# A two-block transformer kernel: mLSTM scores and FoX denominators on the whole matmul array, and new written-out orders for two stages

## The reference, cut to what matters

```python
def _mixer(h, lb, w_in, b_in, a_q_g, a_k_g, b_conv_w, out_g, w_out):
    z = h @ w_in + b_in
    ...
    oa = _fox_attention(qa, ka, _heads(a_v, A_HEADS), ca)            # 8 heads of 64
    qk = jax.nn.silu(_causal_dwconv(b_qk, b_conv_w))
    ob = _mlstm_chunkwise(...)                                       # 4 heads of 64
    oc = _hgrn2_chunkwise(jax.nn.silu(_heads(c_q, C_HEADS)), logf, _heads(c_i, C_HEADS))  # 4 heads of 64
    ya = _rms(_merge(oa), g_a.reshape(A_HEADS, HEAD_DIM)).reshape(bsz, t, A_DIM)
    ...
    return jnp.concatenate([ya, yb, yc], axis=-1).astype(h.dtype) @ w_out
```

```python
        z = jnp.einsum("bhqd,bhkd->bhqk", qb, kb) * scale
        log_1m = jnp.where(valid, jax.nn.log_sigmoid(-z), 0.0)
        log_a = jax.nn.log_sigmoid(z) + lax.cumsum(log_1m, axis=3, reverse=True) - log_1m
        a = jnp.where(valid, jnp.exp(log_a), 0.0)
        outs.append(jnp.einsum("bhqk,bhkd->bhqd", a.astype(v.dtype), v[:, :, :kend]))
```

## Time and profile before

| what | value |
|---|---|
| median of 3 runs | 1684.35 us (1683.88 to 1684.54) |
| profiled execution | 1683.83 us |
| its span on the core | 1682.1 us |
| PE busy | 1669.3 us (99%), 7812 instructions |
| PE weight loads busy | 1328.1 us (79%) |
| DVE busy | 882.9 us (52%) |
| ACT busy | 661.8 us (39%) |
| POOL busy | 136.8 us (8%) |
| chain that ended last | PE 97%, DVE 2%, ACT 1% |

### The profile page before, as it was taken

One profiled execution on the slowest core, in us unless ns is written; L12 is line 12 of the kernel. 1 busy time (PEld: TensorE's weight loads), 2 busy tenths in 40 slices (PEclk: granted clock), 3 DMA queues, 4 the chain that ended last, 5 costly groups with the idle time before them and its releaser, 6 DMA issues.

```text
span 1682.1 us, 19174 instructions
## 1 busy us (share of the span) xinstructions
PE 1669.3 (99%) x7812; PEld 1328.1 (79%) x7812; DVE 882.9 (52%) x1161; ACT 661.8 (39%) x972; POOL 136.8 (8%) x161
## 2 busy tenths in 40 slices
PE   9999999999999999999999999999999999999999
PEld 7878877788888778888888877777666888888887
DVE  5436744555554354444443337766545677777321
ACT  5344333333553243233222334255574544444211
POOL 0000000121210010000000220212100200000000
PEclk9999999999999999999999999999999999999999
DMA  6222232232453123323323322412203232233321
GB/s 261 88 77 87 76 101 76 76 99 90 163 164 124 38 78 98 94 94 101 98 90 102 99 101 88 164 64 65 74 26 125 88 101 96 93 100 99 102 94 57
DMA packets 47463, 164.28 MB, mean 98 GB/s; under 512 B 5056, under 2 KB 5184, under 8 KB 47056
## 3 DMA queue, kind: packets, MB, share of 16 engines
q1 hardware_dynamic: 46192, 158.88, 28.6%
q0 software_dynamic: 896, 3.70, 0.7%
q10 hardware_dynamic: 288, 0.48, 0.1%
HBM read 158.81 MB, written 4.23 MB: 97 GB/s over the span
## 4 chain that ended last, share of the span: by engine, by line
PE 97%; DVE 2%; ACT 1%; issue 0%; DMA 0%; POOL 0%; SPq 0%; DVEq 0%; ACTq 0%; POOLq 0%
PE pst L382 95%; PE pst L547 1%; PE pst L830 1%; DVE XL L1584 0%; DMA X<-xT 0%; DVE qx L1804 0%; DVE WL L1572 0%; POOL acc L2283 0%; ACT WH L951 0%; DVE ML L1580 0%; PE pst L671 0%; ACT Sx L951 0%; DVE X L1789 0%; PE pst L621 0%; ACT XH L951 0%
## 5 line engine op out<-in xcount | busy, mean ns | idle before, releaser
L382 PE MATMUL pst<-XH,WH 128*128 128x512 f32 x1320 | 528.4, 400 | 0.0
L382 PE MATMUL pst<-XH,WL 128*128 128x512 f32 x1320 | 514.6, 390 | 0.0
L382 PE MATMUL pst<-XL,WH 128*128 128x512 f32 x1320 | 514.2, 390 | 0.0
L1572 DVE TENSOR_TENSOR WL<-raw,WH 128x1024 fp32r<-128x1024 f32 x276 | 341.8, 1239 | 312.3 <-ACT WH L951 311.8
L951 ACT ACTIVATE WH<-raw 128x1024 fp32r<-128x1024 f32 (+1 forms) x278 | 291.3, 1049 | 356.8 <-PE pst L382 351.1
L382 PEld LDWEIGHTS pst<-XH,WH 128*128 128x128 f32 x1320 | 247.8, 188 | 66.4 <-issue 16.5
L382 PEld LDWEIGHTS pst<-XH,WL 128*128 128x128 f32 x1320 | 247.7, 188 | 52.5
L382 PEld LDWEIGHTS pst<-XL,WH 128*128 128x128 f32 x1320 | 248.0, 188 | 51.9 <-issue 3.4
L382 PE MATMUL pst<-HH,WH 128*128 128x512 f32 x352 | 136.9, 389 | 0.0
L382 PE MATMUL pst<-HL,WH 128*128 128x512 f32 x352 | 136.9, 389 | 0.0
L382 PE MATMUL pst<-HH,WL 128*128 128x512 f32 x352 | 136.9, 389 | 0.0
(11 more groups left out here) (252 smaller groups left out, 1789.6 us busy)
## 6 DMA issues: line engine op xcount, KB each, us to landing
raw<-wst SPq DMA_DIRECT2D x276, 512.0 KB, 3.6
X<-xT SPq DMA_DIRECT2D x7, 512.0 KB, 7.2
xs<-X SPq DMA_DIRECT2D x1, 2048.0 KB, 9.3
nC<-cd POOLq DMA_DIRECT2D x4, 512.0 KB, 7.9
X<-xs SPq DMA_DIRECT2D x2, 1024.0 KB, 5.6
outT<-X SPq DMA_DIRECT2D x8, 256.0 KB, 4.4
qx<-memT SPq DMA_DIRECT2D x1, 1024.0 KB, 5.0
gt<-cd POOLq DMA_DIRECT2D x1, 1024.0 KB, 6.3
```

The lines of the kernel that those rows point to most:

```text
L382: return nc.tensor.matmul(out, lhs, rhs, start=start, stop=stop)
L1572: vec.tensor_tensor(WL[:, i % NHL, :], raw[:, i % NRAW, :], WH[:, i % NHL, :].bitcast(F32), ALU.subtract).then_inc(wl, 1)
```

## The change

**Scores over the whole array.** A new tile `kz` holds the keys of each mLSTM head on their own 64 partitions and zeros on the other 64. POOL fills it with zeros once, before it sets `bv1`. The key half of `bqk_silu` on ACT becomes two instructions of 64 partitions that write into `kz`. A score matmul takes all 128 partitions of `kz` and `bqk`. Since `bqk` still holds the second head's queries then, the outputs go to a new tile `yb`.

**Denominators over the whole array.** `den` loses one copy. ACT's square writes every denominator 64 times into `Sx[:, s, 1, :]`, 512 columns instead of 8, and waits first until the last values are read. PE adds them with four matmuls of 128 columns by 128 instead of eight of 64.

**Orders.** `mixer_order` is spelled out, and `heads_order` is another string. The needs are the same.

```diff
-        den = sb("den", [P, 2, 2, 8], stack=st)
+        den = sb("den", [P, 2, 8, 1], stack=st)
+        pad_ = sb("pad_", [P, 11], stack=st)
+        kz = sb("kz", [P, 2, 2, T], stack=st)
+        yb = sb("yb", [P, 2, T], stack=st)
...
-        mixer_order = weave(
-            {"main": (0, 1, mixer_steps), "stick00": (-0.0593, 0.481, 20), ...
+        mixer_order = spelled(
+            "macamamc5mc5mca5maca6mamcma7mca4ma6mcma2ma4ma8ma4mc3mca5ma2mcmc3mcma5ma3macmac5mc5mc4mc6mc7mbc2mb10mdmdb4mdb5m...
...
-            "21mgm2gm2g5mgm2gmg3m2gmg2m2g2mgm2g2mgmgmgmgm2g2m2gmg4m...
+            "22mgm4g7m3gm2g3mg3mg2m2g4m5g2mgmgm2gmgm2g4m2gmgmgmgmgmg2mgmh...
...
                 mm(ps[b1][:, :], halves, Sx[:, s, 0, :], True, False)
                 for x, i in enumerate((3, 2, 1, 0)):
-                    for e in range(2):
-                        d = den[:, s, 1, 2 * x + e:2 * x + e + 1].to_broadcast([P, 64])
-                        ins = mm(ps[b1][64 * e:64 * e + 64, i * P:(i + 1) * P], d, ident, False, x == 3)
+                    ins = mm(ps[b1][:, i * P:(i + 1) * P], Sx[:, s, 1, x * P:(x + 1) * P], ident, False, x == 3)
...
-                            mm(ps[6][:, 0:w], bqk[po:po + 64, 2 + pt, j * P:(j + 1) * P], bqk[po:po + 64, pt, j * P:T]).then_inc(l_p, 1)
+                            pe.wait_ge(ones_ok, 1)
+                            mm(ps[6][:, 0:w], kz[:, pt, h % 2, j * P:(j + 1) * P], bqk[:, pt, j * P:T]).then_inc(l_p, 1)
...
-                        run(ACT.Silu, bqk[:, m, :], bqk[:, m, :]).then_inc(bq_a, 1)
+                        if i == 0:
+                            run(ACT.Silu, bqk[:, m, :], bqk[:, m, :]).then_inc(bq_a, 1)
+                        else:
+                            act.wait_ge(ones_ok, 1)
+                            run(ACT.Silu, kz[0:64, half, 0, :], bqk[0:64, m, :])
+                            run(ACT.Silu, kz[64:P, half, 1, :], bqk[64:P, m, :]).then_inc(bq_a, 1)
...
-                run(ACT.Square, den[:, s, 1, :], den[:, s, 0, :], scale=(64 * EPS) ** 0.5).then_inc(n_a[s], 1)
                 act.wait_ge(f_y[s], 4 * pn + 4)
+                d = Sx[:, s, 1, :].rearrange("p (h d) -> p h d", d=64)
+                run(ACT.Square, d, den[:, s, :, :].to_broadcast([P, 8, 64]), scale=(64 * EPS) ** 0.5).then_inc(n_a[s], 1)
                 run(ACT.Square, Sx[:, s, 0, :], ystk[:, s, :]).then_inc(n_a[s], 1)
...
-                    run(ACT.Copy, bqk[po:po + 64, pt, :], ps[7][0:64, :]).then_inc(l_a, 1)
+                    run(ACT.Copy, yb[po:po + 64, pt, :], ps[7][0:64, :]).then_inc(l_a, 1)
...
+            gp.memset(kz[:, :, :, :], 0.0)
             gp.memset(bv1[:, :, :, 64:P], 1.0).then_inc(ones_ok, 1)
```

More of the change, by code:

```diff
@@ L322, in yy_src @@
         def yy_src(m):
-            return aq[:, m, :] if m < 4 else bqk[:, m - 4, :] if m < 6 else cq[:, m - 6, :]
+            return aq[:, m, :] if m < 4 else yb[:, m - 4, :] if m < 6 else cq[:, m - 6, :]
         Z_SLOT = [4, 5, 6, 7, 0, 1, 2, 3]
         mixer_steps = 2 * (8 + 4 * 2 + 4 * 6 + 4 * 2 + 24 + 24)
-        mixer_order = weave(
-            {"main": (0, 1, mixer_steps), "stick00": (-0.0593, 0.481, 20), "stick01": (0.577, 0.996, 20), "stick10": (-0.0412, 0.676, 20), "stick11": (0.65, 1.01, 20)},
-            {("stick01", 0): (("stick00", 20),), ("stick11", 0): (("stick10", 20),)})
+        mixer_names = {"m": "main", "a": "stick00", "b": "stick01", "c": "stick10", "d": "stick11"}
+        mixer_needs = {("stick01", 0): (("stick00", 20),), ("stick11", 0): (("stick10", 20),)}
+        mixer_order = spelled(
+            "macamamc5mc5mca5maca6mamcma7mca4ma6mcma2ma4ma8ma4mc3mca5ma2mcmc3mcma5ma3macmac5mc5mc4mc6mc7mbc2mb10mdmdb4mdb5mdmbdm2d2bd3md2mb6mbmdbmbdbd9mbd7mbd2mdbm"
+            "bd3m2bmdmd6mb2md8mdb2m",
+            mixer_names, mixer_needs)
         out_order = weave({"main": (0, 1, 16), "mem": (0.343, 0.761, 18)}, {})
@@ L347, in program @@
         heads_order = spelled(
-            "21mgm2gm2g5mgm2gmg3m2gmg2m2g2mgm2g2mgmgmgmgm2g2m2gmg4mgm3gm2gm2g2m2hm2h3mh5mhmahmhma2hmhamahmhahmamahmha2mahmam2h3mhmama2hacm2ach2amcahcmcamhcmchmchmb"
-            "cmhcbcmhbc2mbhmbhbhmcbcmbmhmchm2cm2bm2cbmlb2dlmbdlbdm2dlb2mdlblmdbldmdlbmdmldl2d2l2mlbld2mlmdldmdldl2ml2mlml2m2lm2lml2ml2mlm",
+            "22mgm4g7m3gm2g3mg3mg2m2g4m5g2mgmgm2gmgm2g4m2gmgmgmgmgmg2mgmh2m3h2mh2ma2hmhma2hmhama2hmamhah2mamhamahmhah4mha2macam2acm2ahcmhmahamcmchbhch2mcmhb2chc2mb"
+            "cmhbc2bhmch2cbmh2mbhmchbcbmcbmbcml2dmbldbldm2dlmbmldmlbdlbdmdlbmdmldl2dlmlmbdmd2lmlmdmdldl2ml2mlm2lm2l2mlm2l2mlml2m",
             heads_names, heads_needs)
@@ L1464, in fox @@
                         act.wait_ge(f_v[s], 2 * n + e + 1)
-                        d = den[:, s, 0, 2 * x + e:2 * x + e + 1]
+                        d = den[:, s, 2 * x + e, :]
                         run(ACT.Exp, S, S, scale=-1.0, bias=smx[:, s, e:e + 1], accum_out=d).then_inc(f_ex[s], 1)
@@ L2216, in mlstm @@
                     if po:
-                        src = bqk[:, pt, :]
+                        src = yb[:, pt, :]
                         yield
```

## The result

The changed kernel takes 1670.87 us (median of 4 runs, 1670.55 to 1671.40) against 1684.44 us for the kernel before (4 runs, 1683.88 to 1685.28) on the same chip: a ratio of 0.9922, 95% interval 0.9909 to 0.9934. That is 13.6 us less. The profiled execution took 1670.88 us, 12.95 less than that of before.

What follows compares the result with a forecast made beforehand. PE was taken to bound all stages. Changes of shape -11.9, end of the heads +1.65, waits that go -1.5, new waits +0.8 sum to -10.95, giving 1673.4 us; own range 1671 to 1676.5, with rivals 1671 to 1679.

Steps and rivals of the forecast that it cites:

- changes of shape, mixer: In the mixer, PE's changes of array shape fall from 61 to 40, taking 3.9 us off.
- changes of shape, heads: In the heads, PE's changes of array shape fall from 129 to 89, taking 8.0 us off.
- the end of the heads: Last FoX sum to first `w_out2` matmul: 0.95 not gained, 0.5 longer chain, 0.2 product behind; 1.65 us back.
- waits that go: Three PE waits in the first 200 us of the heads (0.7, 0.7, 0.5) shrink: about 1.5 us off.
- half clock: Seven matmuls after the first `w_out2` start run at 1.2 GHz, losing 1.47 us; forecast to stay, so 0.
- The main step: Mixer and heads: each change of array shape costs PE 0.175 (128x64) or 0.205 us (64x128); fewer changes, 11.9 us off.
- The tail heals: Rival, 8%: at the end of the heads the clock isn't lowered, 1.5 us more go: 1671.4.
- the tight place of the mixer: Transposes of a 384-key block stand about 4.9 us behind its scores; PE waits there for 0 to 0.5 us.
- The 0.8 for new ones: New PE waits in mixer and heads where a step moved closer to its cause: 0.8 us, bounds 0 and 3.
- Terms put at nothing: Whole-array scores and denominators, ACT's larger squares, the key's Silu in two instructions, POOL's zeros: each forecast to cost 0.

Runs made afterwards that it cites:

- untile: Kernel before with only the edits putting mLSTM scores and FoX denominators on the whole array, both orders as before: 1681.03 us against 1684.03, ratio 0.9982.
- the extra products: Kernel before with one more 128-column product in each of 44 first-FFN up-projection tiles: 1696.97 us (whole array), 1712.57 (64x128), 1710.38 (128x64), against 1684.51.

## Why the prediction was right, and where it was short

| step of the prediction | forecast | measured |
|---|---|---|
| changes of shape, mixer | -3.9 | -3.9 to `HH` |
| changes of shape, heads | -8.0 | about -6.9, an estimate: 40 at 0.16 to 0.19, as by `untile` and the extra products |
| the end of the heads (not gained, longer chain, product behind) | +1.65 | about -0.1 |
| waits that go, less new ones ahead of the FoX sum | -0.7 | about -1.6, what is left of that stretch's -7.79 without 27 changes (4.7) and the moved work (1.5); PE's waits there are 2.95 before and 1.4 after |
| half clock | 0 | -1.5 |
| new waits at 1310 | 0 | +1.2, in some executions 0 |

- **The main step held.** The price read from two places in the timeline, times counted changes, gave the mixer to 0.1 us. By its own experiment the price is 10% lower. The 21 changes then make 3.5 and not 3.9, so the fit to 0.1 us is in part luck, and 0.4 of the mixer's gain is not accounted for.
- **The step that failed is the end of the heads.** The prediction said that five changes there are not gained (0.95). `untile` shows exactly that: 7.63 us before and with it. It added 0.5 for a longer chain; it is 0.24, though with more work in it. But it left out what the printed order showed: 1.5 us of matmuls move *into* the stretch that waits for the chain, and only 0.2 out of it. There they cost 0.24 at most, and they go from the stretch ahead, where PE is the bound. The term is 0.95 + 0.24 - 1.3 = -0.1, not +1.65. This and the half clock are the two largest misses, 3.2 us together; without either of them the result would have been inside the range.
- **The half clock** was taken as staying "as PE idles in the same place", with 8% for the other case. The place is the same, the idle time is not: 0.98 and 0.79 for 1.41. Had I taken the moved work into account, I would have seen the idle time shrink too, so both misses have the same root. The rival *The tail heals* comes closest to the result (1671.4), and by its mechanism, but its argument "that idle time gets no shorter" is the one that failed. Before's half clock is also not fixed: its executions differ by 3 us with it.
- **Waits that go**: 1.5 was right in kind. Of the three rows two are gone, and the 0.7 for `Sx`, which was two waits, is down to one of 0.2. The one new wait of note ahead of the FoX sum is 0.4 for `ystk`, and the tight place of the mixer does not wait. The 0.8 for new ones was too much there.
- **The new wait** came at 1310 us, in a stage that the change does not touch, because a projection that starts closer behind its chain has less room. I had looked for new waits only where the order was changed.
- **The range** of 1671 to 1676.5 is not what the bounds of the terms add up to. With the bounds stated they give 1671.7 to 1677.6, so the result is 0.8 below them.
- **Terms put at nothing** were nothing: whole-array scores take 604 ns an instruction at 512 columns, not over 645, no FoX sum waits for ACT's squares, and nothing waits for POOL's zeros, which take 1.80 us. The second Silu instruction was nothing only with the new order.

## What to carry to other kernels

Where one engine is the bound and short matmuls of another array shape stand between long ones, read the price of an excursion from starts in the timeline, then put excursions of several streams together; put a matmul that has no partner in the other half on the whole array. Sort every moved instruction by whether the stretch it leaves and the one it enters are bound by that engine: work moved into a stretch that waits for a chain is nearly free (1.3 us for 0.25 here), and work saved there is no gain. After such a change look at the waits downstream of it too, and at idle times just ahead of long matmuls, since here they cost twice, once as waiting and once as a lower clock.

## What was not expected of the hardware

- Six useless products (1.3 us) in an idle time made the kernel 1.6 us faster in the median, by keeping the granted clock at 1.00 where it was 0.60. The unfilled kernel kept it in three of 22 executions, and its times span 3.2 us, in three groups by their mean clock.
- One DVE and one POOL instruction that start 0.04 us apart: either may be the one that takes longer (DVE 0.75 to 1.87, POOL 1.29 to 1.86), and between two executions of the changed kernel, in different sets of runs, it is another. With two losses against none, the end of the program was 1.28 us apart. A difference of this size between two executions need not be the code's.
- A short float32 product on the whole array between projections costs 0.28 us for its two passes of 0.11.
